# A gated recurrence: decays by matmuls of token-wise log decays with a 0/1 matrix, and one pair of score banks instead of two

## The reference

```
f = lb + (1.0 - lb) * sigmoid(z);  k = 1.0 - f;  log_f = log(f)
def step(state, (qi, ki, vi, gi)):                # a chunk of tokens
    bcum = cumsum(gi)                             # gi = log_f, per feature
    o_inter = (qi * exp(bcum)) @ state
    decay[t, s] = exp(bcum[t] - bcum[s]) for t >= s else 0
    scores[t, s] = sum over features of qi[t] * ki[s] * decay[t, s]
    o_intra = scores @ vi
    state = state * exp(blast) + (ki * exp(blast - bcum))^T @ vi
    return state, o_inter + o_intra
```

## Time and profile before

| | us |
|---|---|
| median of 3 runs | 3494.91 |
| lowest, highest | 3493.25, 3501.12 |
| the profiled execution, its own time | 3495.85 |
| its span, from first to last instruction | 3494.5 |
| mean granted TensorE clock, of full speed | 0.942 |

### The profile page before, as it was taken

The page is one execution under the profiler, slowest core; times in us unless marked ns, Lnnn a source line. Parts: engine busy times, 40 slices in busy tenths (PEclk is TensorE's granted clock), DMA queues, the critical chain, the costliest instruction groups (busy, mean ns, idle before and its releaser), DMA issues.

```text
span 3494.5 us, 41938 instructions
## 1 busy us (share of the span) xinstructions
PE 3147.5 (90%) x17442; PEld 2270.0 (65%) x17442; DVE 1470.9 (42%) x3004; ACT 882.2 (25%) x1740; POOL 323.7 (9%) x594
## 2 busy tenths in 40 slices
PE   6988899999999999798688899999999788689998
PEld 4657456666644666687545788888566577448886
DVE  2122222333223146477854332442716475643444
ACT  2011211111122144333222221111315333232222
POOL 0000000000000000345510000000100144300001
PEclk9999899999999996899799999999998899789999
DMA  4433321222222210132341112111111010213222
GB/s 170 134 110 109 104 66 37 55 54 55 61 78 85 61 31 1 41 91 67 98 145 61 52 57 73 58 51 49 73 54 31 16 31 19 73 60 109 89 93 72
DMA packets 225897, 242.28 MB, mean 69 GB/s; under 512 B 5440, under 2 KB 189868, under 8 KB 224428
## 3 DMA queue, kind: packets, MB, share of 16 engines
q1 hardware_dynamic: 225708, 239.60, 21.3%
HBM read 232.24 MB, written 7.34 MB: 69 GB/s over the span
## 4 chain that ended last, share of the span: by engine, by line
PE 80%; DVE 10%; ACT 5%; issue 3%; POOL 1%; DMA 1%; SPq 0%; ACTq 0%; DVEq 0%; POOLq 0%
PE PS L1718 73%; PE PS L1722 4%; PE PS L1927 2%; ACT AR L171 1%; DVE AR L2424 1%; PE PS L1904 1%; ACT L169 1%; DVE AR L2660 1%; ACT EX L171 1%; ACT WC L171 1%; DVE STAT L2596 1%; DVE AR L2415 1%; POOL AR L2701 1%; DVE EX L2647 0%; DVE AC L2652 0%
## 5 line engine op out<-in xcount | busy, mean ns | idle before, releaser
L1718 PE MATMUL PS<-WR,HT 128*128 128x256 f32 (+3 forms) x3920 | 1121.3, 440 | 9.0 <-ACT AR L171 6.6
L1718 PEld LDWEIGHTS PS<-WR,HT 128*128 128x128 f32 x3920 | 682.2, 193 | 360.6 <-issue 193.6
L1718 PE MATMUL PS<-HI,WC 128*128 128x512 f32 (+1 forms) x2112 | 570.1, 357 | 22.3 <-DVE EX L2647 12.5
L1718 PEld LDWEIGHTS PS<-HI,WC 128*128 128x128 f32 x2112 | 378.7, 191 | 81.1 <-issue 13.1
L1718 PE MATMUL PS<-AR 128*64 128x64 f32 (+8 forms) x3756 | 332.3, 277 | 108.3 <-POOL AR L2701 59.5
L1718 PEld LDWEIGHTS PS<-AR 128*64 128x64 f32 (+5 forms) x3756 | 288.4, 180 | 170.1 <-issue 87.4
L1718 PE MATMUL PS<-LO,WC 128*128 128x512 f32 (+1 forms) x1056 | 377.0, 357 | 0.0
L1718 PE MATMUL PS<-HT,WR 128*128 128x256 f32 (+3 forms) x1168 | 362.9, 465 | 10.4 <-DMA WR<-in_w_in 4.8
L171 ACT ACTIVATE AR<-PS 128x256 f32<-128x256 f32 (+3 forms) x362 | 154.4, 456 | 745.7 <-PE PS L1718 591.4
L2641 DVE TENSOR_TENSOR WC<-WR,WC 128x1024 fp32r<-128x1024 f32 x132 | 161.3, 1225 | 405.4 <-ACT WC L171 405.4
L1718 PE MATMUL PS<-WC,AC 128*128 128x512 f32 x1320 | 318.8, 397 | 13.3 <-DVE AR L2660 11.5
(11 more groups left out here) (234 smaller groups left out, 2623.1 us busy)
## 6 DMA issues: line engine op xcount, KB each, us to landing
WR<-in_w_ffn_in SPq DMA_DIRECT2D x44, 1024.0 KB, 6.8
WR<-in_w_in_b SPq DMA_DIRECT2D x54, 512.0 KB, 5.8
WR<-in_w_mod SPq DMA_DIRECT2D x12, 2048.0 KB, 7.9
WR<-in_w_mod SPq DMA_DIRECT2D x24, 1024.0 KB, 5.3
WR<-in_w_ffn_out SPq DMA_DIRECT2D x22, 1024.0 KB, 4.9
WR<-in_w_in SPq DMA_DIRECT2D x40, 512.0 KB, 4.3
WR<-in_w_out SPq DMA_DIRECT2D x8, 2048.0 KB, 8.5
WR<-in_w_in_a SPq DMA_DIRECT2D x8, 1024.0 KB, 5.2
```

What stands on the lines that cost most here:

```text
L1718: mm = lambda o, l, r, start, stop: e.o.matmul(o, l, r, start=start, stop=stop, skip_group_check=True)
```

## The change

The log decays stay token-wise. TensorE turns them once per head and direction (new kind `hp0`: six transposes into `hturn` banks, ScalarE copies them back over the log decays), after VectorE's scan, which now writes its cumulated values to the buffer of weighted queries. The exponents of all levels are then a product: the turned log decays of a tile, tokens on partitions, times a table of zeros and ones (`k_lev`) that says which tokens lie between a column and the middle of its block. `hl1` becomes a step per tile: two matmuls of 384 columns over 64 partitions each (levels of 32 and below, one half of the tile each, to two banks) and one of 128 columns over all 128. ScalarE takes three exponentials per tile directly from PSUM. The seven subtractions on VectorE and on GpSimd are gone.

The matmuls' banks, 2 and 3, are `H.exps`, a ring of one; `H.pair` is a ring of one, banks 0 and 1. One buffer for masked scores fewer (two instead of three) makes room for the table. A class `Ahead` holds the units of all heads in one list and begins tiles up to two units ahead also across heads; `recur` weighs a unit two yields ahead of its scores, and multiplies u + 1 after the reduction of u.

```diff
+    def between(n, h, rev):
+
+        t_, c_ = np.arange(n)[:, None], np.arange(n)[None, :]
+        mid = c_ // (2 * h) * 2 * h + h
+        late = (t_ >= mid) & (t_ < c_ + (not rev))
+        early = (t_ < mid) & (t_ >= c_ + (not rev))
+        return np.where(c_ >= mid, late, early)
...
-            both.update(X=Ring(*[late(7 * 256) for _ in range(3)]), M=Ring(*[late(1024) for _ in range(2)], *products), A=Ring(*weights))
+            lev = early(1024)
+            both.update(X=Ring(*[late(7 * 256) for _ in range(3)]), M=Ring(late(1024), *products), A=Ring(*weights),
+                        levels=lev, lev=[lev[:, 512 * d:512 * d + 512] for d in range(nd)])
...
+                for a in range(0, nt, 4):
+                    e = min(nt, a + 4)
+                    while H.turn.full():
+                        yield
+                    j, bk, until = H.turn.take()
+                    m = P.add("hp0", H, d, a, e, bk, until, P.count["hp1"] + 1)
+                    H.turn.done(j, ("hp_l", m))
+                H.turned[d] = ("hp_l", m)
                 n = P.add("hp1", H, d, kh[0:K, 0:H.nt * 128], kh_until, dec, dec_until, qh[0:K, 0:nt * 128], qh_until)
...
+            def begin(self, upto):
+
+                while self.tiles <= upto and self.tiles < 2 * len(self.units):
+                    (H, u), t = self.units[self.tiles // 2], self.tiles % 2
+                    if H.units[u][1] not in H.turned or t == 0 and H.b["X"].full():
+                        break
+                    levels_begin(H, u, t)
+                    self.tiles += 1
...
-                if u + 1 < len(H.units):
-                    levels_weigh(H, u + 1)
-                if u + 2 < len(H.units):
-                    levels_begin(H, u + 2)
-                yield
-                if u + 1 < len(H.units):
-                    levels_multiply(H, u + 1)
+                n = first + u
+                ahead.begin(2 * n + 1)
+                ahead.weigh(n)
+                ahead.multiply(n)
+                ahead.weigh(n + 1)
+                ahead.begin(2 * n + 5)
                 yield
                 levels_reduce(H, u)
                 carried_end()
+                yield
+                ahead.multiply(n + 1)
+                ahead.begin(2 * n + 6)
                 yield
...
-            hpair, hturn, hout = Ring(pair(0), pair(2)), banks(4, 6) if both else banks(4, 6, 7), banks(5)
+            hpair, hexp, hturn, hout = Ring(pair(0)), Ring(pair(2)), banks(4, 6) if both else banks(4, 6, 7), banks(5)
...
+            def hl1(n, H, i, d, t, xb, x_until, E, until):
+                lt, lev = H.dirs[d][1][:, 128 * (i + t):128 * (i + t) + 128], H.b["lev"][d]
+                e.wait_ge(*H.turned[d])
+                e.wait_ge(*H.b["lev_need"])
+                e.wait_all(until)
+                for hf in range(2):
+                    mm(E[:, hf, 0:384], lt[64 * hf:64 * hf + 64, :], lev[64 * hf:64 * hf + 64, 0:384], True, True)
+                mm(E[:, 0, 384:512], lt, lev[:, 384:512], True, True).then_inc(sem("hl_b"))
...
+            def hp0(n, H, d, a, b, bk, until, scan):
+                e.wait_ge("hp_f", n)
+                e.wait_ge("hp_c", scan)
+                e.activation(H.dirs[d][1][:, 128 * a:128 * b], bk[:, 0:128 * (b - a)], ACT.Copy).then_inc(sem("hp_l"))
...
-            def hl1(n, H, i, d, xb, until):
-                x = xb[0:H.K, :]
+            def hl1(n, H, i, d, t, xb, x_until, E, until):
+                x3 = xb.rearrange("p (l n) -> p l n", l=7)
                 e.wait_ge("hl_b", n)
-                e.wait_ge("hl_k", n)
-                e.activation(x, x, ACT.Exp).then_inc(sem("hl_e"))
+                e.wait_all(x_until)
+                e.activation(x3[:, 0, 128 * t:128 * t + 128], E[:, 0, 384:512], ACT.Exp)
+                for hf in range(2):
+                    o = x3[:, 1:7, 128 * t + 64 * hf:128 * t + 64 * hf + 64]
+                    x = e.activation(o, E[:, hf, 0:384].rearrange("p (l n) -> p l n", l=6), ACT.Exp)
+                x.then_inc(sem("hl_e"))
...
-            def hl1(n, H, i, d, xb, until):
-                k, lg, rev, order = H.dirs[d]
-                K = H.K
-                x3 = xb[0:K, :].rearrange("p (l n) -> p l n", l=7)
-                lo, hi = 128 * i, 128 * i + 256
-                e.wait_ge(*H.cum[d])
-                e.wait_all(until)
-                for l in range(7):
-                    h = 64 >> l
-                    v = lambda a: a.rearrange("p (n t h) -> p n t h", t=2, h=h)
-                    b4 = v(lg[:, lo:hi])
-                    ref = b4[:, :, 1, 0:1] if rev else b4[:, :, 0, h - 1:h]
-                    s = tt(v(x3[:, l, :])[:, :, 0 if rev else 1, :], b4[:, :, 0 if rev else 1, :], ref.broadcast_to([K, 128 // h, h]), ALU.subtract)
-                s.then_inc(sem("hl_b"))
```

More of the change, by code:

```diff
@@ L834, in build, with rec_bufs @@
         ths[3] = norm_end(ths[3])
-        def rec_bufs(K, V, nt, nd, mask, early, late, products, weights, decays):
+        def rec_bufs(K, V, nt, nd, mask, lev_need, early, late, products, weights, decays):
             TT = 128 * nt
@@ L905, in prepare @@
                 H.turn.done(j, ("hp_u", m))
-            if before:
-                while not before.begun:
-                    yield
-                H.units = units(H)
-                for u in range(2):
-                    while H.b["X"].full():
-                        yield
-                    levels_begin(H, u)
-                    yield
-                while not before.multiplied or H.pair.full():
-                    yield
-                levels_weigh(H, 0)
-                levels_multiply(H, 0)
@@ L920, in levels_first, with __init__, weigh, multiply @@
-        def levels_first(H):
-            H.units = units(H)
-            levels_begin(H, 0)
-            levels_begin(H, 1)
-            levels_weigh(H, 0)
-            levels_multiply(H, 0)
+        class Ahead:
+            def __init__(self, heads):
+                self.units, self.tiles = [(H, u) for H in heads for u in range(len(H.units))], 0
+            def begin(self, upto):
[5 more added lines that the diff above has]
+                    self.tiles += 1
+            def weigh(self, n):
+                if n < len(self.units) and self.tiles > 2 * n + 1:
+                    H, u = self.units[n]
+                    if "weighed" not in H.lv[u]:
+                        levels_weigh(H, u)
+            def multiply(self, n):
+                if n < len(self.units):
+                    H, u = self.units[n]
+                    if "weighed" in H.lv.get(u, ()) and "multiplied" not in H.lv[u]:
+                        levels_multiply(H, u)
@@ L1484, in third_set, with sums_fetched @@
                 yield
-            filling = itertools.chain(project(0), prepare(heads[0]), project(1), third_set())
+            def sums_fetched(n=n, hb=hb):
+                P.add("ld", "mask", hb[0]["levels"], A["k_lev"], n, ())
+                return iter(())
+            filling = itertools.chain(project(0), itertools.chain.from_iterable(f() for f in (sums_fetched, lambda: prepare(heads[0]))), project(1), third_set())
             due = [0]
@@ L1499, in build @@
                 P.add("ld", "mask", hb[0]["mask"][d].bitcast(U16), A["k_mask"][:, 512 * d:512 * d + 512], P.count["fence"], ())
-            levels_first(heads[0])
-            preps = [prepare(heads[h + 1], heads[h]) for h in range(3)] + [iter(())]
+            ahead = Ahead(heads)
+            ahead.begin(3)
+            ahead.weigh(0)
+            ahead.multiply(0)
+            preps = [prepare(heads[h + 1]) for h in range(3)] + [iter(())]
             early_w[2] = load(pieces(2)[0], 8, 128, by_quarter(2)[0])
```

89 lines of the change are left out of this document (40 added, 49 removed).

## The result

| | us |
|---|---|
| the changed kernel, median of 4 runs | 3523.86 |
| lowest, highest | 3522.15, 3525.46 |
| the kernel before, same chip, median of 4 | 3497.14 |
| ratio, with its 95% interval | 1.0076 [1.0059, 1.0094] |
| the profiled execution's span, its granted clock | 3520.8, 0.951 |

The changed kernel is 0.76% slower, 26.7 us. The prediction said 3484 (3458 to 3516): the wrong direction, and outside its range.

What follows compares the result with a forecast made beforehand. TensorE has most work in the recurrences but does not set the pace alone, waiting for GpSimd, VectorE and ScalarE. 77 + 11 + 6 - 46 - 32 - 27 = -11 us from 3495.85 us gave 3484 us, range 3458 to 3516.

Steps and rivals of the forecast that it cites:

- Both recurrences, the reading of before: Both recurrences: TensorE has most work but is idle 146 us, at a granted clock of 0.87 and 0.86.
- One tile 1.07 us, 86 in all: Exponent matmuls on TensorE: 1.07 us per tile, eighty tiles 86 us, of which +77 us not hidden.
- 9 us hidden in the openings: Start of each recurrence: four tiles per layer fall into TensorE's idle time, opening chain as long as the old; 9 us hidden.
- hp0 +11: Turning the log decays among the projections: 96 transposes on TensorE count in full, +11 us.
- handoff +6: Tiles waiting for ScalarE when it is blocked behind VectorE's scan: 12 places at 0.5 us, +6 us.
- Waits for weighed levels -46: Recurrences beyond the openings: TensorE's waits for the decay-weighted levels all go, -46 us.
- late engines -32: Recurrences: two thirds of TensorE's 48 us of waits for late VectorE or ScalarE go, -32 us.
- Clock -27: Recurrences: half of the 54 us that TensorE loses at the lower clock comes back, -27 us.
- handoff rival: One bank pair makes tiles wait for ScalarE, ScalarE for VectorE's scan; slower, 3530 us at worst, half of it 3512; chance 0.25.
- No side by side: The 64-partition tile matmuls don't overlap; a tile costs 1.6 us, 72 tiles 38 us more, 3522 us; chance 0.05.
- TensorE-bound throughout: In the recurrences all late waits and most of the slow clock go: -43 us, 3452 us; chance 0.14.
- The draw: Recovered time equals the added matmuls, as only half the late waits and less clock come back: 3495 us; chance 0.20.

Runs made afterwards that it cites:

- after: The changed kernel itself, as measured against the kernel before: 3523.86 us, ratio 1.0076.
- e14: The changed kernel without hp0: log decays not turned, so the exponents are wrong but the other work is the same; 3508.32 us.
- rung "-5": Step from e15 (3513) to e14 (3508): subtractions gone, in their place the chain of matmul, exponential from one bank pair, weighing; -5 us.
- e1: The kernel before with only the change's new order of units; old subtractions, two score pairs and three masked-score buffers kept; 3467.99 us.
- e2: As e1, new order with the old subtractions, but with a single pair of score banks; 3472.31 us.
- e15: e2 plus the tiles' matmuls, made of constants into free banks that nothing reads; 3513.21 us.
- e3: The changed kernel with each tile's matmuls in one bfloat16 pass, on the high half of the log decays alone; 3481.49 us.
- e4: The changed kernel with the three exponentials of each tile made twice; 3569.40 us.
- e6: The changed kernel with the three matmuls of every tile made twice; 3609.49 us.
- e9: e1 with two masked-score buffers, plus log-decay transposes and ScalarE's copies into an unread buffer; the scan waits for the transposes; 3507.54 us.
- e10: As e9 but without ScalarE's copies: only the 96 transposes, for which the scan waits; 3507.44 us.
- e7: New order, one score pair; forward direction's exponents by matmuls as in the changed kernel, backward direction's by the old subtractions; 3499.95 us.
- e11: The changed kernel with two exponentials per tile instead of three; 3521.91 us.
- e12: e1 with two buffers for masked scores instead of three; 3467.17 us.
- e13: e12 plus 96 transposes of a constant at the place of hp0, waiting for nothing and not awaited by the scan; 3472.73 us.
- e8: e1 plus log-decay transposes and ScalarE's copies of them into the buffer of the keys; the scan waits for the copies; 3527.75 us.
- e5: The changed kernel with log decays kept as two bfloat16 parts and tile matmuls in two bfloat16 passes; 3501.79 us.

## Why the prediction was wrong

Two steps of the sum failed. The tiles' matmuls were priced at 86 us and hold TensorE for 108, the largest single error. And the opening chain was taken "to be as long as the old", so that 9 us of tiles would be hidden there; the openings grew by 7.5 us instead. The recovered time, by contrast, came nearly as forecast, but mostly for another reason than the one given.

- **Both recurrences, the reading of before.** It held: TensorE has most work, gaps of 146 us, the clock at 0.87 and 0.86.
- **One tile 1.07 us, 86 in all.** Too low. At the full clock a tile holds TensorE 1.17 to 1.26 us, and in the openings, at the lower clock, 2.3 to 2.4. All 80 are 108 us: +22. Nine of these are the eight tiles of the two openings (17.5 us instead of 8.6), 13 are the other 72, at 1.26 us each. The pairing itself held: records of 384 columns start in twos, 6 to 7 ns apart, and each two take 0.42 us, as the assumed 0.83 for a pair has it. But the 128-column matmul behind them takes 0.33 instead of 0.24.
- **9 us hidden in the openings.** The timeline of after's first opening:

```profile
1448.62 1.33 PE L1757 MATMUL PS<-AR,EX 64*128 64x384 f32 x6 [2.73 <-ACTq L2048]
...
1452.43 2.38 PE L1757 MATMUL PS<-AR,EX 64*128 64x384 f32 x6 [2.47 <-ACT AR L181]
...
1455.94 2.38 PE L1757 MATMUL PS<-AR,EX 64*128 64x384 f32 x6 [1.13 <-ACT AR L181]
...
1459.44 2.38 PE L1757 MATMUL PS<-AR,EX 64*128 64x384 f32 x6 [1.13 <-ACT AR L181]
...
1461.75 1.55 PE L1757 MATMUL PS<-AR 128*64 128x64 f32 x24
```

  Four tiles go through one bank pair in turn, 3.5 us each at the slow clock, and the unit's scores stand behind all four in TensorE's queue. The first scores come 13.2 and 13.8 us after the mark instead of 9.7 and 9.7: 7.5 us lost where I had booked 9 as hidden. I had named this as a way to be wrong, and given it no price.
- **hp0 +11 and handoff +6.** e14 gives 16 for hp0 with its places, 3 of them in the stretch between the recurrences. For the handoff's +6 no run gives a number; its waits of 21 us are part of the rung "-5".
- **Waits for weighed levels -46, late engines -32.** As accounts of gaps they held: the gaps fell by 73 us, 78 were foreseen. As causes they did not. The weighing was no longer waited for beyond the openings with the order alone (e1 and e2), and most of the rest of the gaps fills with any work on TensorE (e15). The prediction treated "TensorE's gaps shrink by 78" and "TensorE gets 88 us more" as two entries of a ledger. They are largely one event.
- **Clock -27.** It came as foretold (0.93 and 0.94; I had asked for 0.92 or more). TensorE's other records in the two recurrences, the same 5320 in both kernels, fell from 415 to 390 us: -25. But with e15's unread matmuls they fell too, from e2's 411 to 395.
- **The sizes.** From -11 to the measured +26.7 are 37.7 us: 22 for the tiles, 2 for the clock, 8 for the gaps (they fell by 73 us, where 78, the 9 hidden and the 6 of the handoff make 81), less 1 for hp0's transposes in the recurrences, and 6 for the stretches outside them, which the sum had left as they were (+7.0 and -1.1).
- **Rivals.** The time is near that of the handoff rival (3530 at worst), but not by its mechanism: by it the gaps should have come back under another name and the clock given back half, and neither happened. "No side by side" is refuted by the starts in twos. "TensorE-bound throughout" is refuted in an instructive way: TensorE works 88% of the two recurrences, up from 75%, and the kernel is not faster that way. The draw is nearest to what came, recovered time eaten up by added matmuls, but not by its terms either: it let half of the late waits stay, where the gaps fell nearly as forecast and the matmuls were dearer. That the time came out near two of the rivals' is no merit of theirs.

What stays open: how much the subtractions' end gives and how much the new chain takes inside the rung "-5"; beyond the openings' 9 us no run separates the two. And the stretch between the recurrences is 4 us longer in after, e3, e4, e6, e9 and e10 (1005.1 to 1005.5) than in e1, e2, e7, e11 to e15 (1000.4 to 1002.2); in e8 it is 1010.7 and in e5 1004.0. All of the longer ones turn the log decays behind ScalarE's logarithm for every direction (hp0), and the others don't, but for e11, which does too, and e7, which does for half. So hp0 alone does not decide it.

## What to carry to other kernels

A gap on the busiest engine and work added to it are not two independent entries: first ask what closing the gaps by order alone would bring, run that, and price the added work against what is left. Moving work from an engine busy 74% of the time to one busy 75% pays only if the first is still waited for once the order has been mended. A step that opens a stage has no cover: four tiles through a single bank pair cost 3.5 us each there, at the slow clock, against 1.17 us in the steady part.

## What the runs showed of the hardware that I had not expected

- A tile of mixed shapes costs more than its columns. The float32 tile (four records of 384 columns in twos over 64 partitions, two of 128 over all) holds 1.17 to 1.26 us at the full clock; by the columns of the earlier trace rows it would be 0.97. That the change of shape is the reason was not tried by itself. The tile of one bfloat16 pass, 0.34 us, is cheaper than half a float32 tile by far: 3.4 to 1.
- The granted clock followed how full TensorE was, whatever filled it: e2, with 126 us of gaps, had 0.88 and 0.86; e15, with the same dependencies and unread matmuls in the gaps, 0.93 in both stretches.
- Between the recurrences there is a stretch of 50 us at a low clock, 0.64 to 0.73 in before, after, e1, e7, e10 and e11. In after, and in e11's profiled run, which was 6 to 8 us faster than its other three:

```profile
2706.00:2756.00 50.00, 45.64 (x206) 33.30 (x205) 34.43 (x69) 22.41 (x49) 1.82 (x1) 0.64 0.00 1
```

```profile
2704.90:2754.90 50.00, 45.52 (x223) 33.34 (x222) 38.98 (x78) 25.08 (x55) 1.81 (x1) 0.70 0.00 1
```

  The same steps, a clock of 0.64 against 0.70, and 17 records more done. What decides it stays open. The whole stretch between the recurrences took 1005.4 us in the first of these and 1000.7 in the second, though their edit does not touch it. So a difference of 5 us between two of these kernels may come from there and not from the edit. The clock alone does not tell which it will be: e1 had 0.64 too, and 1001.4 us.
